# Decode attention in one inference step: block selection ahead of the window branch, bias by one-hot products, lists loaded from two queues

## The chip, the core and the metric

One core of a Trainium2 chip runs the whole program in one launch. The metric is device time in microseconds (us) of one execution; the time of a kernel is the median of its runs. A core has TensorE (PE in the profile), VectorE (DVE), ScalarE (ACT), GpSimd (POOL) and SyncE (SP). Each has its own instruction queue, and they meet only at semaphores. Sixteen DMA engines are shared by all; a load is issued by the queue of SP, ACT or POOL.

## What is computed

The kernel is one layer of a hybrid decoder, run for a prompt of 1024 tokens and for eight sequences (`B = 8`) that each add one token to a cache of 8192. Only the attention of those eight new tokens is touched by the change. It has three branches, each with a bias that depends on distance; `BG = 16` pairs of sequence and key/value group, four query heads each:

```python
s_c = einsum(q, kc) + bias_c;  p_c = softmax(s_c);  o_c = p_c @ vc          # 511 compressed blocks
imp = sum(p_c, heads) @ block_cover                                          # importance of 129 blocks of 64 tokens
score = where(valid, where(forced, BIG, imp), NEG)                           # first, last and current block forced
_, idx = top_k(score, 16)                                                    # a list of 16 blocks per pair
k_sel, v_sel = ks_blk[b, g, idx], vs_blk[b, g, idx]                          # gathered from the paged cache
s_s = einsum(q, k_sel) + table[rel_bucket(qpos - kpos)];  o_s = softmax(s_s) @ v_sel
s_w = einsum(q, kw) + bias_w;  o_w = softmax(s_w) @ vw                       # window of 512
o = gate_c * o_c + gate_s * o_s + gate_w * o_w
```

The bias depends on the distance in buckets; beyond 790 tokens it is one value, the last bucket.

## The kernel before

The program is a row of stages with a barrier of all engines between two; `decode_attention` (L1878) is one of them, after the attention of the prompt and before `merge`. Nothing of the next stage runs in it. Rows of the score matrix `S` (64 partitions) are sequence and head; its columns are 512 compressed, 512 window and 1024 selected keys.

**SP** (L1930) issues all plain loads: compressed keys `kcT` (2 MB in one), window rows `win` (8 of 512 KB), the page table `pti`, gates `gt`, compressed values `vc`, and later, per list, the one row of the new token into the gathered block (L1945), after the list's gathers have landed.

**POOL** (L1949) makes constants, then issues 16 indirect gathers of bias rows into `bsel` (L1969), then 8 indirect gathers per list into `kvs` (L1977): 128 rows of 1 KB each, keys and values of both groups. `kvs` has two slots; a slot is free when PE has turned it (`s_sT`) and ACT has copied its values (`s_vs`).

**PE** (L2094): scores of the compressed keys (L2099); then per sequence the window's keys are turned (`win_turn`, L2107) and multiplied (L2115); importance (L2118); two small products that spread indices (L2120, L2121); per list 8 turns (`sel_turn`, L2131) and two score products (`sel_scores`, L2141), each two rows of the trace; then 16 turns of `S` (L2154) and 256 value products (L2167), all 128 of one group (partitions 0 to 63 of the bank), then all of the other (64 to 127). A product is two instructions in the trace.

**DVE** (L1980), in this order: window copies (L1993), compressed softmax (L1995 to L2000), selection (L2003 to L2012), block numbers to row numbers by 16 pairs of one-hot and sum (L2022, L2025), row numbers `gidx` (L2040), window maximum, per list two copies of turned keys (L2052), then maximum, factors and scaling of all three branches (L2055 to L2072), and the last copy into `oaT` (L2077). ACT does the exponentials (L2084, L2086, L2092) and the copies of values (L2090).

## Time and profile before

| | us |
|---|---|
| median of 3 runs | 3674.04 (3670.31 to 3681.82) |
| the profiled execution, device time | 3669.99 |
| its span in the trace | 3668.4 |
| the stage `decode_attention`, 2023.41 to 2332.70 of the span | 309.3 |

Over the whole span TensorE is busy 83%, and the granted clock is 0.873 of full speed. In this stage it is another picture, so the shares of the page say little here: the stage has to be read in stretches, with the timeline for the starts and the stretches' table for busy time, granted clock and DMA. "Granted clock" is the share of 2.4 GHz that TensorE got: 0.50 is its lower level of 1.2 GHz, 1.00 the upper.

### The profile page before, as it was taken

The numbers are of one execution on the slowest core, as the hardware profiler recorded it, in microseconds if no ns is written. First come the engines' busy times: TensorE is split into PE (matmuls) and PEld (weight loads), VectorE is DVE, ScalarE is ACT, GpSimd is POOL, SyncE is SP. The second block draws the span as 40 slices with busy tenths as digits, with TensorE's granted clock in tenths as the row PEclk, the third lists the DMA queues.
The fourth block names the chain that finished last, engine by engine and source line by source line (L and its number), as shares of the span: only waits on it lengthen the run. The fifth ranks groups of instructions, "written<-read, shape, count | busy, mean of one in ns | idle before, by whom it ended". The sixth has DMA issues, their size and how long they took to land. (4 is left out here: it accounts for less than half of the span.)

```text
span 3668.4 us, 48382 instructions
## 1 busy us (share of the span) xinstructions
PE 3050.1 (83%) x17167; PEld 2645.7 (72%) x17167; DVE 1508.2 (41%) x3336; ACT 1134.4 (31%) x2011; POOL 620.3 (17%) x983
## 2 busy tenths in 40 slices
PE   4799979998497649599999356899986799999996
PEld 3677758786395449577777123888875799999995
DVE  3456546564414640144555311111133444444446
ACT  3577757774421211143344000111112211111112
POOL 6556546650001000000000374000000000000000
PEclk9899989998798859777788655699998899999998
DMA  9778768871413233300000332411122211111111
GB/s 120 103 114 117 113 100 122 119 109 59 161 42 116 95 103 127 100 18 12 6 12 0 111 105 63 139 46 40 29 87 99 69 46 57 34 51 51 34 34 46
DMA packets 268889, 276.13 MB, mean 75 GB/s; under 512 B 51738, under 2 KB 224270, under 8 KB 268088
## 3 DMA queue, kind: packets, MB, share of 16 engines
q1 hardware_dynamic: 209470, 180.94, 18.2%
q0 software_dynamic: 43520, 67.82, 11.5%
q10 hardware_dynamic: 15738, 25.40, 3.9%
q8 instruction: 79, 1.29, 0.2%
q14 instruction: 82, 0.67, 0.1%
HBM read 241.17 MB, written 36.71 MB: 76 GB/s over the span
## 5 line engine op out<-in xcount | busy, mean ns | idle before, releaser
L232 POOL DMA_DIRECT2D raw<-in_cache_nsa_kv x768 | 457.0, 595 | 348.1 <-issue 307.1
L2193 PE MATMUL bank<-u2H,fwiH 128*128 128x344 f32 x1056 | 338.3, 320 | 39.2 <-DVE fwiL L2560 39.2
L405 ACT ACTIVATE cy<-bank 64x512 f32<-64x512 f32 x512 | 303.0, 592 | 116.9 <-PE bank L286 109.9
L2193 PE MATMUL bank<-u2H,fwiL 128*128 128x344 f32 x1056 | 337.9, 320 | 0.0
L2193 PE MATMUL bank<-u2L,fwiH 128*128 128x344 f32 x1056 | 337.7, 320 | 0.0
L2193 PE MATMUL bank<-cxH,cwH 128*128 128x512 f32 x768 | 324.5, 423 | 3.3 <-DVE cxL L517 3.3
L2193 PE MATMUL bank<-cxH,cwL 128*128 128x512 f32 x768 | 307.0, 400 | 0.0
L2193 PE MATMUL bank<-cxL,cwH 128*128 128x512 f32 x768 | 306.8, 399 | 0.0
L2193 PEld LDWEIGHTS bank<-u2H,fwiH 128*128 128x128 f32 x1056 | 199.5, 189 | 39.7 <-issue 39.7
L2193 PEld LDWEIGHTS bank<-u2H,fwiL 128*128 128x128 f32 x1056 | 199.2, 189 | 0.0
L2193 PEld LDWEIGHTS bank<-u2L,fwiH 128*128 128x128 f32 x1056 | 198.7, 188 | 0.0
L2193 PEld LDWEIGHTS bank<-cxH,cwH 128*128 128x128 f32 x768 | 147.5, 192 | 51.6 <-issue 15.0
L2568 DVE TENSOR_TENSOR fhm<-bank,fsl 128x344 f32<-128x344 f32 x66 | 34.1, 517 | 344.0 <-ACT fsl L2543 344.0
L286 PE MATMUL bank<-ident,raw 128*128 128x128 f32 x1024 | 140.4, 282 | 42.2 <-DMA raw<-in_cache_nsa_kv 39.9
L2193 PE MATMUL bank<-guH,gwgH 128*128 128x344 f32 x480 | 160.9, 335 | 14.7 <-DMA guL<-uL_d 14.7
L2193 PEld LDWEIGHTS bank<-cxH,cwL 128*128 128x128 f32 x768 | 146.5, 191 | 35.2
L2184 DVE SCALAR_TENSOR_TENSOR xT<-bank,modT,xT 128x344 f32<-128x344 f32 (+1 forms) x264 | 148.6, 570 | 53.2 <-PE bank L2193 53.2
L286 PEld LDWEIGHTS bank<-ident,raw 128*128 128x128 f32 x1024 | 124.6, 146 | 63.5 <-issue 42.8
L2193 PE MATMUL bank<-fhH,fwoL 128*128 128x344 f32 x528 | 169.7, 321 | 0.0
L2193 PE MATMUL bank<-fhH,fwoH 128*128 128x344 f32 x528 | 168.9, 320 | 0.0
L2193 PE MATMUL bank<-fhL,fwoH 128*128 128x344 f32 x528 | 168.9, 320 | 0.0
L2193 PEld LDWEIGHTS bank<-cxL,cwH 128*128 128x128 f32 x768 | 147.5, 192 | 25.9
(479 smaller groups left out, 6411.3 us busy)
## 6 DMA issues: line engine op xcount, KB each, us to landing
raw<-in_cache_nsa_kv POOLq DMA_DIRECT2D x768, 64.0 KB, 8.2
fwi<-in_w_ffn_in SPq DMA_DIRECT2D x44, 512.0 KB
raw<-in_cache_nsa_kv SPq DMA_DIRECT2D x256, 64.0 KB
wada<-in_w_ada ACTq DMA_DIRECT2D x8, 2048.0 KB
fwo<-in_w_ffn_out SPq DMA_DIRECT2D x22, 512.0 KB
gwg<-in_w_in SPq DMA_DIRECT2D x20, 512.0 KB
mwada<-in_w_ada SPq DMA_DIRECT2D x4, 2048.0 KB, 9.0
mwada<-in_w_ada_final SPq DMA_DIRECT2D x4, 2048.0 KB, 8.0
```

The source lines that it names most:

```text
L232: eng.dma_start(raw[8 * q:8 * q + 8, t % 2, nt], pages[bass.ds(at[n], 1), :, :, P * kv:P * kv + P] .rearrange("o n s c -> (o n) s c")).the ...
L286: mm = pe.transpose(k.bank[6 + odd][:, P * nt:P * nt + P], raw[:, t % 2, nt, 2 * j + odd, :], k.ident[:, :])
L405: ins = act.activation(y[HD * odd:HD * odd + HD, kk % 3, 0:2, g, 0:HP], k.bank[6 + odd][HD * g:HD * g + HD, :].rearrange("p (i r) -> p r i ...
L2184: dve.scalar_tensor_tensor(out=x, in0=bank[:, 0:w], scalar=k.modT[:, bass.ds(gate + c, 1), 0:1].rearrange("p o b -> p (o b)"), in1=x, op0= ...
L2193: mm = pe.matmul(out, a[x], b[y], start=start and n == 0, stop=stop and n == 2)
L2568: dve.tensor_tensor(hm[:, u % 2, :], k.bank[2 * (u % 2) + 1][:, 0:GT], sl[:, u % 2, :], ALU.mult).then_inc(s_hm, 1)
```

## The change

Only `decode_attention` is changed.

- **Order.** The compressed softmax, the selection and the row numbers now come ahead of the window branch on PE and DVE. Small conversions that don't depend on the selection are done before it. The 16 pairs of one-hot and sum are staggered by one. The window's turned keys are copied by ACT instead of DVE. `kcT` comes in four loads; `win` and `vc` are issued by ACT.
- **Bias.** The 16 gathers of `bsel` are gone. 28 small loads bring the bias of the 14 nearest blocks (`near`) less the far value, a one-hot matrix `oh` says which block stands where, and 16 products (L2210) add the bias into the score banks after the first list. The far value is the same for all keys of a head and drops out of the softmax.
- **Lists.** Blocks 0 to 7 of a list are loaded by SP, with a page address read from `tix` into registers (8 plain loads of 64 rows per list, L1966); blocks 8 to 15 by 4 indirect gathers of POOL (L1999), the last of 64 rows. The new token's row is loaded by SP beside them. `kvs` has three slots instead of two.
- **Other branches during the loads.** Window maximum, exponential and factors, the first 8 turns of `S` and the value products of the compressed and window branches (128 products over lists 6 to 13) stand between the lists. The selected branch's own value products (128) stay behind the last list. In both, the two groups now alternate product by product.

On SP, the queue of a list. Before, this was one row of 1 KB per list; the whole queue of the stage was:

```order
L1932 DMA kcT<-kcT_d 128x4096
L1934 DMA dwin<-out_win_sample 128x4x256 x8
L1937 DMA dpti<-in_page_table 1x64 x16
L1939 DMA dgt<-smalltok_d 8x3 x8
L1940 DMA vc<-vc_d 128x4096
L1945 DMA dkvs<-out_kv_sample 1x256 x16
```

Now, from the last pair of bias loads to the first of list 0's blocks (ISA is the address arithmetic):

```order
L1948 DMA dnear<-biasrev_d 8x64
L1949 DMA dfar<-biasrev_d 8x2
L1958 DMA dkvs<-out_kv_sample 1x256
L1962 TENSOR_LOAD dtix
L1966 ISA
L1966 DMA dkvs<-in_cache_nsa_kv 64x256
```

The last two rows come eight times per list, and the four rows from L1958 on begin each of the 16 lists.

On DVE, the front of the stage, before:

```order
L1986 COPY qpad<-qTs 64x8x4 x2
L1993 COPY dwT<-bank 128x512 x8
L1995 ISA dS,dmx<-bank,bias_cmp 64x512
L1995 ISA dmx 64x1
L1996 TENSOR_SCALAR dnm<-dmx 64x1
```

and now:

```order
L2009 COPY qpad<-qTs 64x8x4 x2
L2012 CAST diota<-diti 16x128
L2013 CAST dcolf<-dcoli 128x1
L2014 CAST dwho<-dwi 128x64
L2015 TENSOR_SCALAR dprow<-dcolf 128x1
L2016 TENSOR_SCALAR dprow<-dprow 64x1
L2019 TENSOR_SCALAR dtokb<-dpti 16x64 x2
L2022 ISA dS,dmx<-bank,bias_cmp 64x512
```

The maximum over the compressed scores (L1995, now L2022) no longer stands behind eight copies of the window branch.

On PE, the end of the stage, before (the last three rows come 16 times):

```order
L2131 MATMUL bank<-ident,dkvs 128x128 x8
L2141 MATMUL bank<-dsT,qpad 64x512 x4
L2154 MATMUL bank<-ident,dS 128x64 x16
L2167 MATMUL bank<-dpT,vc 64x4 x4
L2167 MATMUL bank<-dpT,dwin 64x4 x4
L2167 MATMUL bank<-dpT,dvsel 64x4 x8
```

and now, from the last value products that stand between lists:

```order
L2233 MATMUL bank<-dpT,vc 64x4 x8
L2233 MATMUL bank<-dpT,dwin 64x4 x8
L2194 MATMUL bank<-ident,dkvs 128x128 x8
L2204 MATMUL bank<-dsT,qpad 64x512 x2
L2194 MATMUL bank<-ident,dkvs 128x128 x8
L2204 MATMUL bank<-dsT,qpad 64x512 x4
L2221 MATMUL bank<-ident,dS 128x64 x8
L2233 MATMUL bank<-dpT,dvsel 64x4 x128
```

Half of the turns and half of the value products have left the end.

The core of the diff:

```diff
+    RING = 3
+    NEAR = PAST // SEL - 13
...
         def _(sp):
-            sp.dma_start(kcT[:, :, :], k.kcT_d).then_inc(s_kc, 16)
-            for b in range(B):
-                sp.dma_start(win[:, b], k.o["win_sample"]...).then_inc(s_win, 16)
+            for j in range(4):
+                sp.dma_start(kcT[:, 2 * j:2 * j + 2, :], k.kcT_d[:, 2 * j:2 * j + 2, :]).then_inc(s_kc[j], 16)
...
-            sp.dma_start(vc[:, :, :, :], k.vc_d).then_inc(s_vc, 16)
+            for n in range(14):
+                sp.dma_start(near[H * n:H * n + H, :], k.biasrev_d[0:H, SEL * (NEAR + n):SEL * (NEAR + n + 1)]).then_inc(s_bias, 16)
+                sp.dma_start(far[H * n:H * n + H, :], k.biasrev_d[0:H, 0:2]).then_inc(s_bias, 16)
...
             for bg in range(BG):
-                sp.wait_ge(s_ga[bg % 2], 128 * (bg // 2 + 1))
-                sp.dma_start(kvs[64:65, bg % 2, 7, :], new[bg // 2:bg // 2 + 1, 256:512]).then_inc(s_new[bg % 2], 16)
+                r = bg % RING
+                if bg >= RING:
+                    sp.wait_ge(s_sT, 2 * (bg - RING + 1))
+                    sp.wait_ge(s_vs, bg - RING + 1)
+                sp.dma_start(kvs[64:65, r, 7, :], new[bg // 2:bg // 2 + 1, 256:512]).then_inc(s_blk[r], 16)
+                if bg == 0:
+                    sp.wait_ge(s_idx, 3)
+                at = nc.values_load_multi_w_load_instructions(tix[0:1, TOPN * bg:TOPN * bg + 8], ...)[1]
+                for n in range(8):
+                    sp.dma_start(kvs[64 * (n % 2):64 * (n % 2) + 64, r, n // 2, :], tokens[bass.ds(at[n], SEL), 256:512]).then_inc(s_blk[r], 16)
...
         def _(pool):
-            pool.wait_ge(s_bidx, 1)
-            for n in range(TOPN):
-                pool.indirect_dma_start(out=bsel[:, SEL * n:SEL * n + SEL], ...).then_inc(s_bg, 16)
             pool.wait_ge(s_idx, 2)
             for bg in range(BG):
-                if bg >= 2:
-                    pool.wait_ge(s_sT, 2 * (bg - 1))
-                    pool.wait_ge(s_vs, bg - 1)
-                for m in range(8):
-                    pool.indirect_dma_start(out=kvs[:, bg % 2, m, :], ...).then_inc(s_ga[bg % 2], 16)
+                if bg >= RING:
+                    pool.wait_ge(s_sT, 2 * (bg - RING + 1))
+                    pool.wait_ge(s_vs, bg - RING + 1)
+                for m in range(4, 8):
+                    n = P if m < 7 else 64
+                    pool.indirect_dma_start(out=kvs[0:n, r, m, :], ...).then_inc(s_ga[r], 16)
...
         def _(dve):
+            dve.memset(kvs[64:P, :, 7, :], 0.0).then_inc(s_z, 1)
...
-            dve.tensor_scalar(bidx[:, :], k.bank[5][0:64, 0:TOPN], hrow[:, :], None, ALU.add).then_inc(s_bidx, 1)
+            dve.tensor_scalar(tix[:, :], k.bank[6][0:1, 0:BG * TOPN], 0.5, None, ALU.mult).then_inc(s_idx, 1)
+            dve.tensor_tensor(yr[:, :, :], ..., ALU.mult).then_inc(s_ix, 1)
+            for a in range(2):
+                dve.tensor_tensor(oh[:, 8 * a:8 * a + 8, :], k.bank[4 * a][0:112, :]..., ALU.is_equal).then_inc(s_oh, 1)
...
+                if bg == 2:
+                    window()
+                if bg == 3:
+                    window_factors()
+                if bg == 4:
+                    turned(0)
...
         def _(act):
+            for b in range(B):
+                act.dma_start(win[:, b], k.o["win_sample"]...).then_inc(s_win, 16)
+            act.dma_start(vc[:, :, :, :], k.vc_d).then_inc(s_vc, 16)
             act.wait_ge(s_gt, 16 * B)
             act.activation(gt[:, :], gt[:, :], ACT.Sigmoid).then_inc(s_sig, 1)
...
         def _(pe):
+            def values(b, sel):
+                for n in range(8):
+                    for g in range(G):
+                        ...
+                        mm = pe.matmul(k.bank[1 if sel else 4][HD * g:HD * g + HD, 4 * b:4 * b + 4], v,
+                                       pT[:, 8 * sel + n, 8 * b + 4 * g:8 * b + 4 * g + 4], start=(n == 0), stop=(n == 7))
...
             for bg in range(BG):
                 sel_turn(bg)
                 if bg:
                     sel_scores(bg - 1)
+                if bg == 4:
+                    rows_turn(0)
+                if bg >= 6 and bg < 6 + B:
+                    mm = values(bg - 6, 0)
             sel_scores(BG - 1)
+            rows_turn(1)
+            for b in range(B):
+                mm = values(b, 1)
```

## Rows read from the trace of the kernel before

**Rows 1.** Stretches of the stage: busy time, instructions, granted clock, DMA.

```profile
core 0: us, PE busy (x) PEld busy (x) DVE busy (x) ACT busy (x) POOL busy (x), PEclk, DMA share, GB/s
2023.00:2041.00 18.00, 9.56 (x16) 2.66 (x16) 0.37 (x2) 1.28 (x1) 1.77 (x9) 0.72 0.96 331
2041.00:2056.00 15.00, 13.22 (x47) 5.72 (x48) 5.77 (x9) 1.49 (x2) 0.00 (x0) 0.89 0.45 165
2056.00:2107.00 51.00, 3.42 (x9) 0.90 (x6) 16.23 (x66) 1.63 (x4) 24.47 (x27) 0.54 0.11 28
2107.00:2262.00 155.00, 82.22 (x185) 35.72 (x186) 21.60 (x32) 10.08 (x16) 112.16 (x118) 0.50 0.34 101
2262.00:2278.00 16.00, 8.90 (x24) 2.96 (x22) 5.97 (x18) 1.24 (x2) 0.00 (x0) 0.50 0.01 2
2278.00:2333.00 55.00, 54.37 (x512) 54.28 (x512) 0.24 (x2) 0.00 (x0) 0.00 (x0) 0.50 0.00 1
```

**Rows 2.** Timeline of POOL; start, us, line, [idle before <-releaser].

```profile
2074.61 1.00 POOL L1969 DMA_INDIRECT dbsel<-biasrev_d,dbidx  x1 [49.25 <-DVE dbidx L2036]
...
2253.28 0.95 POOL L1977 DMA_INDIRECT dkvs<-in_cache_nsa_kv,dgidx  x1 [0.30 <-issue]
```

**Rows 3.** Line L1977: duration ns min/median/max, first and last start; time to landing.

```profile
L1977 POOL DMA_INDIRECT dkvs<-in_cache_nsa_kv,dgidx x128: 947/953/972, 2094.2 to 2255.8; - x128
...
DMA to landing us min/median/max: 2.6/2.8/3.7
```

**Rows 4.** Timeline, the front of the stage.

```profile
2023.41 0.33 SPq L1932 DMA_DIRECT2D kcT<-kcT_d  x1
...
2030.86 9.56 PE L2099 MATMUL bank<-kcT,qpad 128*64 128x512 f32 x16 [9.74 <-DMA kcT<-kcT_d]
...
2055.77 0.68 DVE L1995 CUSTOM_DVE_ANT_0 dS<-bank,bias_cmp 64x512 f32<-64x512 f32 x1
...
2074.95 0.73 DVE L2040 TENSOR_SCALAR dgidx<-bank,dprow 64x128 uint32<-64x128 f32 x2 [0.63 <-PE bank L2121]
```

**Rows 5.** SP's issues by line: duration ns min/median/max, first and last start.

```profile
L225 SPq TENSOR_LOAD <-pt x32: 692/1069/1367, 2.4 to 777.0; - x32
L232 SPq DMA_DIRECT2D raw<-in_cache_nsa_kv x256: 676/692/7371, 3.3 to 805.4; - x128
L232 SPq DMA_DIRECT2D raw<-in_cache_nsa_kv x2: 676/676/676, 7.1 to 8.0; - x2
L1652 SPq DMA_DIRECT2D strip<-biasfwd_d x8: 333/338/538, 1559.7 to 1890.5; - x8
L1934 SPq DMA_DIRECT2D dwin<-out_win_sample x8: 427/1389/3372, 2023.8 to 2033.9; - x8
L1945 SPq DMA_DIRECT2D dkvs<-out_kv_sample x16: 222/223/237, 2105.7 to 2258.5; - x16
```

**Rows 6.** Timeline of PE: a list's turns and scores; window scores at the upper clock.

```profile
2259.72 1.97 PE L2131 MATMUL bank<-ident,dkvs 128*128 128x128 f32 x8 [4.16 <-DMA dkvs<-out_kv_sample]
...
2265.44 3.64 PE L2141 MATMUL bank<-dsT,qpad 64*64 64x512 f32 x4
...
2050.17 1.07 PE L2115 MATMUL bank<-dwT,qpad 128*64 128x512 f32 x2
```

**Rows 7.** A stretch of the prompt's attention, columns as in rows 1.

```profile
1570.00:1610.00 40.00, 40.00 (x122) 28.57 (x120) 15.02 (x66) 11.75 (x38) 0.00 (x0) 0.50 0.00 1
```

**Rows 8.** Timeline of PE where value products pass from one group to the other.

```profile
2305.10 0.25 PE L2167 MATMUL bank<-dpT,dvsel 128*64 128x4 f32 x1
2305.13 0.25 PE L2167 MATMUL bank<-dpT,vc 128*64 128x4 f32 x1
...
2305.21 0.25 PE L2167 MATMUL bank<-dpT,dvsel 128*64 128x4 f32 x1
```

**Rows 9.** Timeline, the end of the stage.

```profile
2278.10 1.01 PE L2167 MATMUL bank<-dpT,vc 128*64 128x4 f32 x8 [0.78 <-DVE dpT L2075]
...
2332.51 0.19 DVE L2077 COPY oaT<-bank 128x32 f32<-128x32 f32 x1 [54.47 <-PE bank L2167]
```

More of the change, by code:

```diff
@@ L1921, in decode_attention @@
         gidx = k.sb("dgidx", [P, BG, 8], U32, ctx=ctx)
-        bidx = k.sb("dbidx", [64, TOPN], U32, ctx=ctx)
-        bsel = k.sb("dbsel", [64, NSELK], ctx=ctx)
-        kvs = k.sb("dkvs", [P, 2, 8, 256], ctx=ctx)
+        tix = k.sb("dtix", [1, BG * TOPN], I32, ctx=ctx)
+        yr = k.sb("dyr", [BG, TOPN, 64], ctx=ctx)
+        near = k.sb("dnear", [112, SEL], ctx=ctx)
+        far = k.sb("dfar", [112, 2], ctx=ctx)
+        oh = k.sb("doh", [112, TOPN, 64], ctx=ctx)
+        kvs = k.sb("dkvs", [P, RING, 8, 256], ctx=ctx)
         sT = k.sb("dsT", [P, 2, NSELK], ctx=ctx)
@@ L1939, in _ @@
                 sp.dma_start(gt[8 * b:8 * b + 8, :], k.smalltok_d[b, 0:24].rearrange("(h r) -> h r", r=3)).then_inc(s_gt, 16)
-            sp.dma_start(vc[:, :, :, :], k.vc_d).then_inc(s_vc, 16)
+            for n in range(14):
+                sp.dma_start(near[H * n:H * n + H, :], k.biasrev_d[0:H, SEL * (NEAR + n):SEL * (NEAR + n + 1)]).then_inc(s_bias, 16)
+                sp.dma_start(far[H * n:H * n + H, :], k.biasrev_d[0:H, 0:2]).then_inc(s_bias, 16)
             new = k.o["kv_sample"][0].rearrange("b o v g d -> b (o v g d)")
+            sp.wait_ge(s_z, 1)
             for bg in range(BG):
-                sp.wait_ge(s_ga[bg % 2], 128 * (bg // 2 + 1))
-                sp.dma_start(kvs[64:65, bg % 2, 7, :], new[bg // 2:bg // 2 + 1, 256:512]).then_inc(s_new[bg % 2], 16)
-            for j in range(2):
-                sp.wait_ge(s_new[j], 8 * BG)
+                r = bg % RING
[4 more added lines that the diff above has]
+                if bg == 0:
+                    nc.disable_value_cache = True
+                    sp.wait_ge(s_idx, 3)
+                at = nc.values_load_multi_w_load_instructions(
+                    tix[0:1, TOPN * bg:TOPN * bg + 8], engines=(mybir.EngineType.SP,), min_val=0, max_val=POOL * PAGE - SEL,
+                    skip_runtime_bounds_check_because="a page number of the table, by its meaning, and a half of the page")[1]
+                for n in range(8):
+                    sp.dma_start(kvs[64 * (n % 2):64 * (n % 2) + 64, r, n // 2, :], tokens[bass.ds(at[n], SEL), 256:512]).then_inc(s_blk[r], 16)
+            nc.disable_value_cache = False
+            for j in range(RING):
+                sp.wait_ge(s_blk[j], 144 * len(range(j, BG, RING)))
         @block.gpsimd
@@ new lines, in _ @@
+            for bg in range(BG):
+                g, r = bg % 2, bg % RING
+                act.wait_ge(s_ga[r], 64 * (bg // RING + 1))
+                act.wait_ge(s_blk[r], 144 * (bg // RING + 1))
+                act.activation(vsel[:, bg], kvs[:, r, :, P + HD * g:P + HD * g + HD], ACT.Copy).then_inc(s_vs, 1)
+                if bg == 2:
+                    act.wait_ge(s_nm, 2)
+                    act.activation(S[:, 512:1024], S[:, 512:1024], ACT.Exp, bias=nm[:, 1:2], accum_out=ls[:, 1:2]).then_inc(s_exp, 1)
@@ L2094, in _ @@
+            act.wait_ge(s_nm, 3)
+            for a in range(2):
+                ins = act.activation(S[:, 1024 + 512 * a:1536 + 512 * a], k.bank[5 + a][0:64, :], ACT.Exp, bias=nm[:, 2:3], accum_out=ls[:, 2 + a:3 + a])
+            ins.then_inc(s_exp, 1)
         @block.tensor
@@ L2096, in _ @@
             pe.wait_ge(s_qp, 2)
-            pe.wait_ge(s_kc, 16)
             for b in range(B):
+                if b % 2 == 0:
+                    pe.wait_ge(s_kc[b // 2], 16)
                 mm = pe.matmul(k.bank[0][0:64, :], qp[:, 64 * b:64 * b + 64], kcT[:, b, :], start=(b == 0), stop=(b == B - 1))
             mm.then_inc(s_sc, 1)
-            pe.wait_ge(s_win, 16 * B)
+            pe.wait_ge(s_const, 8)
+            pe.wait_ge(s_p, 1)
+            pe.matmul(k.bank[4][0:BG, :], gsel[:, :], S[:, 0:512], start=True, stop=True).then_inc(s_imp, 1)
+            pe.wait_ge(s_ix, 1)
+            pe.matmul(k.bank[6][:, 0:BG * TOPN], k.ones[0:BG, :], tbd[:, :, :].rearrange("p n m -> p (n m)"), start=True, stop=True).then_inc(s_imp, 1)
+            pe.wait_ge(s_ix, 2)
+            for a in range(2):
+                pe.matmul(k.bank[4 * a][0:112, :], k.ones[0:BG, 0:112], yr[:, 8 * a:8 * a + 8, :].rearrange("p n r -> p (n r)"),
+                          start=True, stop=True).then_inc(s_y, 1)
             def win_turn(b):
```

202 lines of the change are left out of this document (111 added, 91 removed).

## The prediction

> **What bounds the kernel now.** I read the stage in stretches first, then the starts of the work that ends each stretch. It runs from 2023.41 to 2332.70 [rows 4, 9], 309.3 us of the span, and four limits follow one another in it.
>
> The front, to 2094.2, moves no cache rows. The compressed scores end on PE at 2030.86 + 9.56 = 2040.42, but DVE starts on their maximum only at 2055.77, because the window's eight copies stand ahead of it in its queue; selection to row numbers then takes until 2074.95 + 0.73 = 2075.68 [rows 4]. POOL's first gather is at 2074.61, and 16 gathers of bias keep it from the lists until 2094.2 [rows 2, 3].
>
> The loop of 16 lists is POOL's: 128 gathers start between 2094.2 and 2255.8 [rows 3], each 0.95 us with 0.30 of idle time between two [rows 2], so 10.06 us a list. DMA engines are busy 0.34 there, PE 82 of 155 us, at granted clock 0.50 [rows 1].
>
> Then the softmax over the selected keys, from 2265.44 + 3.64 = 2269.08 [rows 6] to the first value product at 2278.10 [rows 9]: 9.0 us. Last 512 value instructions in 54.4 us [rows 1], 0.1066 us each, with PE alone.
>
> **The change part by part.** *Front.* DVE no longer waits behind the window: the maximum starts when the compressed scores end. Their keys now share the DMA engines with the window's rows, which ACT issues at the same time. Shared evenly, 2.1 MB of keys arrive with 2.1 MB of others at 331 GB/s [rows 1]: 12.7 us instead of 6.3, so the last quarter lands near 2037 instead of 2030.86, and its four score rows follow, 3.6 us at the lower clock by the four of a list [rows 6], less at the upper: 2040.4, the old end. Without contention it would be 2037; with the loads crowding out the keys, 2044. ACT issues nine loads, at a median 1.39 us [rows 5] some 12.5 us, before the gates' sigmoid and the exponential: done at about 2036, ahead of 2041. Gain 15.3 us. The chain from the maximum to the row numbers, 19.9 us [rows 4], I keep whole: what leaves it and what its staggered pairs hide, 1 to 3 us, stays as margin. First gather 2040.4 + 19.9 + 0.3 = 2060.6; SP, after `tix` and a register load, 2061.7. The bias gathers, 2094.2 - 2074.6 = 19.5 us [rows 2, 3], are gone from POOL. Their replacement: 28 small loads on SP, 0.22 to 0.36 us each [rows 5], 6 to 10 us, behind which only SP's own lists stand, and these wait for `tix` until 2061: nothing. The one-hot matrix on DVE (three operations of about 0.7 to 1.3 us) lies beside PE's window branch: nothing, and if it were late, list 0's scores would be by as much. On PE 16 bias products, 32 instructions of 64 columns at about 0.12 us, an estimate from the 0.107 of rows 1: 3.9 us after list 0.
>
> *Window branch.* It moves behind the selection on PE: 3 us for the one-hot's products, then the 15 us of before (2041 to 2056) [rows 1]; PE reaches list 0 at 2061 + 18 - 1 = 2078. Queued behind it: turns and, on ACT, copies of values of lists 0 to 2, so slots come free late and lists 3 on start some 2 us later than they could.
>
> *Loading a list.* POOL: 4 x 1.25 = 5.0 us. SP: eight loads, a register load, one row. The trace has no load of 64 rows of 1 KB from a register's address. Nearest below: 128 rows of 4 KB with such an address, 0.34 us (L1652); above: 128 pieces of 512 bytes, 0.68 (L232), and these follow one another at 0.9, so 0.2 lies between [rows 5]. I take 0.34 + 0.2, since the pieces are few and long: 8 x 0.54 + 0.22 + 0.1 + 0.69 to 1.07 = 5.5 us. By the upper row: 8 x 0.9 + 1.07 + 0.3 = 8.6. Both ends are under 10.06. Lists by SP alone would end at 2061.7 + 16 x 5.5 + 2 = 2152.
>
> The DMA engines were the lesser concern: at 101 GB/s they are busy 0.34 [rows 1]; a list of 1 MB in 5.5 us is 191 GB/s, below the 331 of the front. The Trainium skill (DMA: Bandwidth & Descriptors, Rules for kernel authors) says that spreading loads over SP, ACT and GpSimd gains no bandwidth, and that two transfers to disjoint halves of the partitions serialize; by that rule a list could not be faster than its bytes allow. At the front's 331 GB/s that is 3.2 us, which would end nothing here.
>
> *PE in the loop.* A list is 1.97 us of turns and 3.64 of scores [rows 6], 5.6 us; that was half hidden under 10.06 and now is as long as the load. Into it come 8 turns (1.0 us) and eight times 32 value instructions. If the two groups run side by side these cost 0.053 each, 1.7 us a list. The trace shows that once, where one group ends: products of the two, 0.03 us apart, each at 0.11 [rows 8]. At the lower clock the loop is 16 x 5.6 + 3.9 + 1.0 + 8 x 1.7 = 108 us. It enters from the window branch at the upper clock, where score rows take half (1.07 for two [rows 6]); I take off 4 us for that. 2078 + 104 = 2182, later than the loads' 2152: PE ends the loop.
>
> *Which clock.* Here the two readings part. In the prompt's attention, with 64-row score products and turns as here, PE was busy 40 of 40 us and the clock stayed at 0.50 [rows 7]; the old loop had 0.50, too, and the value products ran 54 us at 0.50 [rows 1]. I take 0.50.
>
> *End.* Of the 9.0 us, two scalings of `S`, eight turns and one copy of turned rows go, and the exponential is in two parts: 6.6, an estimate. Value products: 256 x 0.053 = 13.7 us instead of 54.4. Last addition 0.4. End of the stage 2182 + 6.6 + 13.7 + 0.4 = 2202.7, before 2332.7: 130 us less. The barrier behind the stage hands all of it on. From the profiled execution, 3669.99 - 130 = 3540; that execution lies 4 us under the median of the runs shown, which gives 3544 against it, and I put the forecast at **3541**.
>
> **Rivals.** *The clock rises.* The loop's work now has hardly a gap. Then a list costs PE about 3 us and the loads end the loop: 2061.7 + 88 + 2 + 2.8 to land, one turn and two lists of scores 4.6, end 20: 2179, 154 us less, **3518**; with SP at POOL's 5.0 us, 3510. For it: the window branch, as dense, came to 0.89 [rows 1]. Against: rows 7. The Trainium skill (TensorE: Matmul & The Clock Gate, Why this matters for your kernels) advises keeping TensorE busy without a break so that it gets the upper clock; by that rule this would be the forecast, and rows 7 speak against it for this mix of shapes.
>
> *Value products don't pair.* Then 0.107 each: 8 x 1.7 more in the loop and 13.7 more at the end, 27 us: **3568**. For it: rows 8 are a few instructions, and here both groups follow in one stream for hundreds. The Trainium skill (the same page, The mechanism) says that a weight load overlaps running products only when the row group differs, and here both groups use all rows; by that rule this is the result. Rows 8 are against it.
>
> *SP's loads are slow.* At 8.6 us a list the loads end the loop: 2061.7 + 138 + 2.8 + 2.0 + two lists of scores 7.3, end 20.7: 2232, 100 us less, **3570**. For it: row L232, the only one that loads the same cache by the same means.
>
> *Slower than before.* SP's issue is held by its queue: the same line L232 took up to 7.37 us [rows 5]. Every list waits for SP, so this decides from 14.9 us a list (2061.7 + 16 x 14.9 + 12.1 + 20.7 = 2332.7), which is 1.5 us an issue besides the 0.2 between. At 2.0 us, 19 us a list, the stage ends at 2399: **3740**. Against: that row stands in a stretch where several queues fill the DMA engines; here they have half their time left.
>
> *Nothing gained.* The stage would have to keep 10 us a list; no row gives a price for that but the last rival at one point.
>
> **How the numbers follow.** Forecast 0.47; clock rises 0.23; no pairing 0.13; SP slow 0.12; slower 0.04; no effect 0.01. The first four are all faster by over 0.3% (11 us, about what a measurement of this kernel can tell from no change): faster 0.95, same 0.01, slower 0.04. The forecast's own spread is the front's +4 and -3, 1 to 3 us of the chain, and the part of the loop at the upper clock, 3525 to 3552. The range takes in the three faster rivals with the bounds of SP's pace, 3508 to 3574; outside lie SP slower still, and two of the late cases together.
>
> **What would show it.** Right: the compressed maximum by 2044, first gather by 2063, no `bsel`; starts of lists 5 to 6 us apart in lists 1 to 5 and near 7.3 in 6 to 13, with PE the one waited for and clock 0.50; SP's loads 0.3 to 0.4 us; last value products 14 us. Clock at 1.00 in the loop shows the first rival, 27 us of last products the second, ACT and PE waiting for SP's loads with gaps of 3 us the third. The forecast is wrong if keys land after 2045, if DVE or ACT hold the slots (a third party I cost at nothing: per list DVE has 21.6 / 16 = 1.4 us, ACT 10.1 / 16 = 0.6 [rows 1], and the window's maximum and factors come to DVE once), or if POOL's gathers slow beside SP's.

## The result

The changed kernel takes 3549.93 us (median of 4 runs, 3538.05 to 3555.70) beside 3672.18 us for the one before on the same chip: a ratio of 0.9658, 95% interval 0.9626 to 0.9691. The forecast was 3541, its range 3508 to 3574. The profiled execution has a span of 3544.3 us. Its decode stage begins at 2028.66 and ends at 2208.76, 180.1 us long; it was 309.3 [rows 4, 9]. The forecast had 179.3.

One thing has to be known for everything below. The code ahead of the stage is the same in all kernels here, yet the stage began anywhere between 2002.85 and 2048.12 us in the profiled executions. A few us in the stage therefore can't be read from the time of a single run; I compare the length of the stage within each profile, from POOL's first memset (`qpad<-`) to the end of DVE's last addition or copy (`oaT<-bank`), and use whole times where there are several runs. The changed kernel's own stage is 180.1 us in one profile and 180.7 in another (changed_again below), so differences of that size are not read.

The stage after, in stretches, with the columns of [rows 1]:

```profile
core 0: us, PE busy (x) PEld busy (x) DVE busy (x) ACT busy (x) POOL busy (x), PEclk, DMA share, GB/s
2028.00:2043.00 15.00, 8.94 (x16) 2.38 (x16) 2.46 (x11) 0.00 (x0) 1.92 (x10) 0.77 0.91 300
2043.00:2066.00 23.00, 3.08 (x4) 0.63 (x4) 14.78 (x58) 3.58 (x5) 0.67 (x1) 0.58 0.49 172
...
2084.00:2094.00 10.00, 8.97 (x65) 5.42 (x64) 4.17 (x7) 1.24 (x3) 6.08 (x7) 1.00 0.45 132
2094.00:2104.00 10.00, 5.77 (x23) 3.16 (x22) 4.01 (x12) 1.97 (x4) 7.56 (x9) 0.87 0.57 166
2104.00:2187.00 83.00, 82.10 (x404) 41.81 (x402) 16.52 (x25) 6.92 (x11) 35.45 (x38) 0.50 0.41 122
...
2194.00:2209.00 15.00, 13.82 (x256) 13.73 (x256) 0.84 (x2) 0.00 (x0) 0.00 (x0) 0.50 0.01 3
```

Against [rows 1], the 51 us in which PE was idle and POOL gathered bias rows have become 23; the 155 us of lists, with PE half idle, are 103, the last 83 of them with PE busy for 82.1 us but at clock 0.50; and the 55 us of value products are 14.

The front after, from the timeline (start, us, engine, line; idle time before it and what ended that in brackets), to be read beside [rows 4]:

```profile
2028.66 0.58 POOL L1973 MEMSET qpad<- 128x576 f32 x1 [130.07 <-POOLq L135]
2028.67 13.45 ACTq L2128 DMA_DIRECT2D dwin<-out_win_sample  x8
...
2033.05 8.94 PE L2158 MATMUL bank<-kcT,qpad 128*64 128x512 f32 x16 [6.08 <-DMA kcT<-kcT_d]
...
2040.06 0.19 PEld L2158 LDWEIGHTS bank<-kcT,qpad 128*64 128x64 f32 x2 [0.80 <-DMA kcT<-kcT_d]
...
2042.14 1.54 ACTq L2129 DMA_DIRECT2D vc<-vc_d  x1
...
2042.41 0.40 DVE L2019 TENSOR_SCALAR dtokb<-dpti 16x64 f32<-16x64 int32 x2 [10.61 <-DMA dpti<-in_page_table]
...
2042.85 0.68 DVE L2022 CUSTOM_DVE_ANT_0 dS<-bank,bias_cmp 64x512 f32<-64x512 f32 x1
...
2043.72 1.28 ACT L2131 ACT_TABLE_LOAD   x1 [34.54 <-issue]
...
2045.24 1.28 ACT L2133 ACT_TABLE_LOAD   x1
...
2047.38 0.15 DVE L2025 TENSOR_SCALAR dmx<-dls 64x1 f32<-64x1 f32 x1 [3.66 <-ACT dS L2133]
...
2065.33 1.07 POOL L1999 DMA_INDIRECT dkvs<-in_cache_nsa_kv,dgidx  x1 [34.57 <-DVE dgidx L2058]
```

The maximum of the compressed scores starts 14.2 us into the stage (32.4 before), the first gather of a list at 36.7 (70.8 before [rows 3, 4]). The scores themselves end at 13.3; the 0.9 us between are the conversion of the page table (L2019), which now stands ahead of the maximum on DVE and waited 10.61 us for its loads. A new wait shows, of 3.66 us: DVE stands until ACT's exponential is through, and ACT comes to it late, behind nine DMA issues, a sigmoid and two table loads.

Issues of a list by line, as in [rows 5] (duration in ns min/median/max, first and last start): the register load, the eight blocks, the new row on SP, and POOL's gathers.

```profile
L1962 SPq TENSOR_LOAD <-dtix x16: 732/751/803, 2065.5 to 2167.8; - x16
...
L1966 SPq DMA_DIRECT2D dkvs<-in_cache_nsa_kv x128: 468/469/1219, 2066.4 to 2174.1; - x128
...
L1958 SPq DMA_DIRECT2D dkvs<-out_kv_sample x16: 249/402/460, 2048.9 to 2167.3; - x16
...
L1999 POOL DMA_INDIRECT dkvs<-in_cache_nsa_kv,dgidx x64: 905/953/1097, 2065.3 to 2164.5; - x64
```

SP's sixteen register loads lie between 2065.5 and 2167.8, so a list costs it 102.3 / 15 = 6.8 us; in the undisturbed lists 6.6 (two loads at 2073.12 and 2079.69). The waits of the stage say who stood for whom (us in total, times, longest):

```profile
POOL dkvs L1999 <- PE bank L2194: 22.6, 8, 5.8
...
SPq L1958 <- PE bank L2194: 1.1, 2, 1.0
```

POOL stood 22.6 us for free slots, SP 1.1: SP ran at its own speed to the end.

PE in the loop and behind it, from the timeline: turns are L2194, scores L2204, bias products L2210, value products L2233.

```profile
2084.73 1.09 PE L2194 MATMUL bank<-ident,dkvs 128*128 128x128 f32 x8
...
2089.70 2.08 PE L2210 MATMUL bank<-dnear,doh 112*64 112x64 f32 x32
...
2095.71 1.93 PE L2204 MATMUL bank<-dsT,qpad 64*64 64x512 f32 x4
2101.82 1.94 PE L2194 MATMUL bank<-ident,dkvs 128*128 128x128 f32 x8 [4.18 <-issue]
2103.68 3.67 PE L2204 MATMUL bank<-dsT,qpad 64*64 64x512 f32 x4
...
2114.65 1.94 PE L2194 MATMUL bank<-ident,dkvs 128*128 128x128 f32 x8 [0.75 <-issue]
...
2120.12 1.02 PE L2233 MATMUL bank<-dpT,vc 128*64 128x4 f32 x16
...
2121.93 1.97 PE L2194 MATMUL bank<-ident,dkvs 128*128 128x128 f32 x8
...
2184.30 3.64 PE L2204 MATMUL bank<-dsT,qpad 64*64 64x512 f32 x4
...
2194.69 13.82 PE L2233 MATMUL bank<-dpT,dvsel 128*64 128x4 f32 x256 [0.78 <-DVE dpT L2090]
```

Lists 0 to 2 have scores of 1.93 us, the upper clock. Then PE catches up with the loads and stands 4.18 us for list 4. The turns and scores behind that wait (2101.82, 2103.68) are at the lower clock, and to the end of the stage each list's scores take 3.64 to 3.67. Lists with value products are 7.3 us apart (2114.65 to 2121.93).

### The profile page after: what moved, and what is told of

It reads as the page before. It is cut to its first block and busy times, and to the rows that moved or that the text cites. A ratio compares the mean times of both kernels' runs of the same rounds, so it can differ in the third digit from the quotient of the medians.

```text
span 3544.3 us, 48834 instructions
## 1 busy us (share of the span) xinstructions
PE 3023.0 (85%) x17201; PEld 2620.6 (74%) x17201; DVE 1505.1 (42%) x3334; ACT 1138.9 (32%) x2021; POOL 544.5 (15%) x904
```

## The experiments

Length of the stage in each profile, by the rule above; whole times where there are several runs.

| run | stage, us | against | difference | whole kernel, us |
|---|---|---|---|---|
| before | 309.3 | | | 3672.18 |
| changed | 180.1 | before | -129.2 | 3549.93 |
| values_apart | 200.0 | changed | +19.9 | 3569.17 |
| before_values_alternate | 283.2 | before | -26.1 | 3645.22 |
| lists_by_pool | 229.1 | changed | +49.0 | 3597.12 |
| sigmoid_late | 177.8 | changed | -2.3 | |
| before_no_bias_gathers | 292.6 | before | -16.7 | |
| window_first | 195.1 | changed | +15.0 | |
| dense_filler | 192.2 | changed | +12.1 | |
| three_fillers | 176.5 | changed | -3.6 | |
| paired_scores | 173.2 | changed | -6.9 | 3541.44 |
| scores_loads_sigmoid | 161.3 | changed | -18.8 | 3530.59 |
| scalar_loads_too | 155.7 | changed | -24.4 | 3528.95 |
| changed_again | 180.7 | changed | +0.6 | 3548.94 |

**Do the value products pair?** The first experiment undoes the alternating order in the changed kernel, the second puts it alone into the kernel before.

```
             def values(b, sel):
-                for n in range(8):
-                    for g in range(G):
+                for g in range(G):
+                    for n in range(8):
```

> The changed kernel with its value products put back in the order of before: all eight of one group, then all eight of the other, so that no two neighbours write different halves of the bank's rows; all else as changed. Theory (the alternating order pairs them): each instruction goes from about 0.054-0.059 us back to the 0.106 us of before; 256 of them stand in the list loop, which PE bounds (+12 us), and 256 behind the softmax (+13.4 us), so the stage is 25 us longer, about 3575 us. Rival (the order brings nothing, the short products of the end come from fewer of them or from another clock): 13.8 us for the 256 at the end as now, the whole within 3 us of the changed kernel.

The last 256 take 21.5 us instead of 13.82 (all of them grouped, then start by start; same columns as above):

```profile
L2233 PE MATMUL bank<-dpT,dvsel 128*64 128x4 f32 x256 | 21.5, 249 | 0.8 <-DVE dpT L2090 0.8
```

```profile
2111.38 0.25 PE L2233 MATMUL bank<-dpT,dwin 128*64 128x4 f32 x1
2111.41 0.25 PE L2233 MATMUL bank<-dpT,vc 128*64 128x4 f32 x1
2111.49 0.25 PE L2233 MATMUL bank<-dpT,dwin 128*64 128x4 f32 x1
```

The ratio to before is 0.97 (0.9668 to 0.9732), the stage 19.9 us longer: the order pays, and the rival falls. The size was 25 and is 20, and the rows show why: where one group's run of 16 instructions meets the next one's, the two run side by side for a few of them (starts 0.03 us apart, then 0.08). In the kernel before such a place came once in 512 instructions [rows 8]; here every 16.

```
-            for g in range(G):
-                for b in range(B):
+            for b in range(B):
+                for n in range(16):
+                    for g in range(G):
...
```

> The kernel before with one part of the change alone: its 512 value products at the end go group by group alternately. Theory: 54.4 us become 512 x 0.054 = 27.6 us, so 3645 us, 27 us less than before. Rival: the pairing needs what else the change made (half of the products early, a sum of two banks); then 54 us stay and the time is that of before.

```profile
2276.85 1.02 PE L2168 MATMUL bank<-dpT,vc 128*64 128x4 f32 x16 [0.78 <-DVE dpT L2075]
...
2302.47 1.85 PE L2168 MATMUL bank<-dpT,dvsel 128*64 128x4 f32 x32
```

It gave 3645.22 us, ratio 0.99 (0.9865 to 0.9934); the 512 products run from 2276.85 to 2304.3, 27.5 us, and their start in the stage moves by 0.8 us only. That is 0.0537 us each; the prediction had 0.053. So 26 us could be had in the kernel before with an exchange of three loops.

**What is SP's half worth?** All gathers by POOL, SP with the new rows only.

```
-                for m in range(4, 8):
+                for m in range(8):
...
-                at = nc.values_load_multi_w_load_instructions(
...
-                for n in range(8):
-                    sp.dma_start(kvs[64 * (n % 2):64 * (n % 2) + 64, r, n // 2, :], tokens[bass.ds(at[n], SEL), 256:512]).then_inc(s_blk[r], 16)
```

> The changed kernel with all 16 lists gathered by POOL (8 gathers of 128 rows each), SyncE loading only the one new row of each list: SyncE's half undone, all else as changed. Theory: POOL needs 8 x (0.953 + 0.30) = 10.0 us a list, more than PE's 7.3, so the loop is bound by loads; the first gather at +36.7 us of the stage, the last issued 160 us later, then landing 2.8, turn 2.0 and scores 1.9 to 3.7, and the 20.9 us of the end as now: stage about 225 to 227 us, 45 us longer than the changed one, about 3595 us. Rival (PE bounds the loop by its clock whatever loads it, and SyncE's half brings little): within 10 us of the changed kernel.

```profile
2157.91 1.97 PE L2185 MATMUL bank<-ident,dkvs 128*128 128x128 f32 x8 [2.68 <-DMA dkvs<-in_cache_nsa_kv,dgidx]
...
2167.89 1.97 PE L2185 MATMUL bank<-ident,dkvs 128*128 128x128 f32 x8 [2.60 <-DMA dkvs<-in_cache_nsa_kv,dgidx]
```

Lists are 10.0 us apart, PE waits for the gathers in each, and the stage is 49 us longer (45 expected; ratio to before 0.9785, 0.9744 to 0.9827). Of the parts that were undone here, SP's half of the lists is the largest.

**What were the bias gathers worth?** The kernel before without them; the bias of the selected blocks is left out, zeros are added.

```
+            pool.memset(bsel[:, :], 0.0).then_inc(s_bg, 16 * TOPN)
             pool.wait_ge(s_bidx, 1)
-            for n in range(TOPN):
-                pool.indirect_dma_start(out=bsel[:, SEL * n:SEL * n + SEL], out_offset=None, in_=brow,
-                                        in_offset=bass.IndirectOffsetOnAxis(ap=bidx[:, n:n + 1], axis=0)).then_inc(s_bg, 16)
```

> The kernel before without its 16 gathers of the bias rows on POOL; the bias of the selected blocks is left out (a buffer of zeros is added instead). Theory: POOL is the bound there, 16 x 1.25 us stood ahead of its first list, so the lists end 20 us earlier and the stage is 289 us instead of 309. Rival (something else of the front end, PE's window products or the index chain, holds the first list): under 10 us gained.

16.7 us, nearer to the theory than to the rival. The first list gather comes at 2087.16 - 2033.82 = 53.3 into the stage instead of 70.8, 17.4 earlier: POOL now waits for the row numbers, which are ready 1.1 us after it began with the bias [rows 2, 4]. The rest is that the 128 gathers are 1.277 us apart there, 1.272 before.

**What is "selection first" worth?** PE's order of before within the changed kernel: the window's turns and products ahead of the importance product.

```
+            pe.wait_ge(s_win, 16 * B)
+            win_turn(0)
...
             pe.wait_ge(s_const, 8)
             pe.wait_ge(s_p, 1)
...
-            pe.wait_ge(s_win, 16 * B)
-            win_turn(0)
```

> The changed kernel with one thing undone, PE's order: the window's turns and products (about 15 us) stand ahead of the importance and index products again, as before the change; loads, lists, values and all other engines' orders as changed. Theory (selection first is worth the window block): the first gather comes at about +50 instead of +36.7 of the stage; PE then has nothing to do while list 0 loads, and the lists, bound by loads up to list 6 and by PE behind it, end 7 to 13 us later: stage 187 to 193 us. Rival (the window block fills time that the first list's landing takes anyway, and PE is the bound of the loop): within 3 us of 180.

```profile
2078.95 1.07 POOL L1999 DMA_INDIRECT dkvs<-in_cache_nsa_kv,dgidx  x1 [50.20 <-DVE dgidx L2058]
```

```profile
2093.82 1.94 PE L2194 MATMUL bank<-ident,dkvs 128*128 128x128 f32 x8 [4.25 <-DMA dkvs<-in_cache_nsa_kv]
2095.69 3.67 PE L2204 MATMUL bank<-dsT,qpad 64*64 64x512 f32 x4
2099.29 3.67 PE L2210 MATMUL bank<-dnear,doh 112*64 112x64 f32 x32
```

First gather at 52.3, near the 50 expected, but the stage is 15.0 us longer where 7 to 13 were expected. The rows show 3.3 us that the expectation didn't have: without the window's block ahead of it, PE enters the lists at the lower clock, and list 0's scores and the bias products take 3.67 us each instead of 1.93 and 2.08. Read with the changed kernel's rows, the block behind the selection does two things: it fills the time of the first loads, and it hands PE on at the upper clock.

**The exponential behind ACT's issues.** The sigmoid and the compressed values' load go behind it.

```
-            act.dma_start(vc[:, :, :, :], k.vc_d).then_inc(s_vc, 16)
-            act.wait_ge(s_gt, 16 * B)
-            act.activation(gt[:, :], gt[:, :], ACT.Sigmoid).then_inc(s_sig, 1)
             act.wait_ge(s_nm, 1)
             act.activation(S[:, 0:512], S[:, 0:512], ACT.Exp, bias=nm[:, 0:1], accum_out=ls[:, 0:1]).then_inc(s_exp, 1)
+            act.dma_start(vc[:, :, :, :], k.vc_d).then_inc(s_vc, 16)
+            act.wait_ge(s_gt, 16 * B)
+            act.activation(gt[:, :], gt[:, :], ACT.Sigmoid).then_inc(s_sig, 1)
```

> The changed kernel with the sigmoid of the gates and the load of the compressed values moved behind the exponential of the compressed scores on ScalarE (the eight window loads stay ahead). Theory: the exponential stood 2.9 us late behind these (load 1.5, table for the sigmoid, sigmoid, table for the exponential 1.3 us); DVE's wait of 3.66 us ahead of the maximum of the sums falls to under 1 us and everything up to the first gather comes about 2.9 us earlier; the stage is 177 us instead of 180. Rival: the exponential then still waits for its table, or the lists' loop takes the gain back: stage 179 to 181 us.

```profile
2028.74 0.72 ACT L2130 ACTIVATE dS<-dS,dnm 64x512 f32<-64x512 f32 x1 [33.94 <-DVE dnm L2023]
...
2029.59 0.15 DVE L2025 TENSOR_SCALAR dmx<-dls 64x1 f32<-64x1 f32 x1 [0.88 <-ACT dS L2130]
```

DVE's wait falls from 3.66 to 0.88 and the stage by 2.3 us. In this profile no table load stands ahead of the exponential any more; the sigmoid's comes later, beside other work.

**What makes the loop's clock?** One dense product that nobody reads behind each list's scores, then three (the diff is of the first; the second has `range(3)`).

```
+                if 1 <= bg < 16:
+                    for _ in range(1):
+                        pe.matmul(k.bank[0][:, :], k.ident[:, :], kcT[:, 0, :], start=True, stop=True)
                 if bg == 4:
                     rows_turn(0)
```

> The changed kernel with one more product of 128 x 128 by 512 columns (the identity by a row of kcT, into a bank that nobody reads) behind the scores of every list from the second on, as work that uses the whole array; nothing else moved. It asks whether the upper clock of lists 0 to 3 can be held. Theory (the low clock of the list loop is lost at the wait of list 4 and isn't won back by what PE does there): the clock is 0.50 from about list 4 to the end as now, a filler costs 1.8 us there (2 x 0.92, the scores' 512 columns) and the loop ends some 20 to 24 us later, stage about 202 us. Rival (it is the sparse work, half of the rows and four-column products, that the low clock follows): with dense work in every list the clock is back at 1.00, a list costs 1.1 + 1.9 + 0.9 + 1.9 = 5.8 us, loads at 6.6 us a list bound the loop, and the stage is 5 us shorter than now, about 175 us.

```profile
2091.84 1.30 PE L2194 MATMUL bank<-ident,dkvs 128*128 128x128 f32 x8 [2.26 <-issue]
2093.07 3.67 PE L2204 MATMUL bank<-dsT,qpad 64*64 64x512 f32 x4
...
2099.91 1.93 PE L2204 MATMUL bank<-dsT,qpad 64*64 64x512 f32 x4
```

```profile
2106.00:2176.00 70.00, 70.00 (x330) 33.47 (x329) 10.80 (x16) 5.04 (x8) 22.64 (x24) 0.50 0.34 100
```

PE was slowed behind a wait again, here of 2.26 us and for list 5, and in the lists with value products one dense product each then didn't bring the upper clock back: 70 of 70 us busy at 0.50. The rival falls as it stood, for the whole loop. But the clock did come back where the dense product, and no value products, stood between two lists: for list 5's scores (2099.91, 1.93 us) and for those of the last two lists, which the changed kernel, without the dense product, runs at 3.64 to 3.67. So the theory's 20 us were too many (12 measured), and what PE computes has a part in it.

> The changed kernel with three products of 128 x 128 by 512 columns that nobody reads behind the scores of every list from the second on (dense_filler had one). At the upper clock a list then costs PE 1.1 + 1.9 + 2.9 + 1.2 = 7.1 us, more than the 6.6 us of a list's loads, so PE has no wait in the loop once it has begun at the upper clock. Theory (the clock falls at PE's wait for loads at list 4 and not for what PE computes): no wait, clock 1.00 through the loop, lists about 7.1 us apart, stage 175 to 190 us. Rival (the lower clock comes in the loop with or without a wait): 1.97 + 3.67 + 6.2 + 1.9 = 13.7 us a list from where it falls, stage 240 to 265 us.

```profile
2066.00:2156.00 90.00, 89.47 (x522) 43.22 (x522) 21.07 (x38) 8.89 (x15) 44.78 (x48) 1.00 0.47 136
```

```profile
2138.76 1.06 PE L2194 MATMUL bank<-ident,dkvs 128*128 128x128 f32 x8 [0.53 <-issue]
```

With 45 useless products the stage is 3.6 us shorter. From list 2 on PE has one wait, of 0.53 us, and the granted clock is 1.00 for 90 us; lists with value products are 6.69 us apart (2098.05 to 2104.74) although each holds 2.8 us of waste. So these lists, with turns, scores and value products, can run at the upper clock, and the rival falls. In the changed kernel it is lost at a wait that PE runs into because at the upper clock it is faster than SP loads. Whether the missing wait or the dense products kept the clock up here, this pair of runs doesn't separate; that one dense product isn't enough in the lists with value products, the first of the two shows. And the run prices the rival "the clock rises" of the prediction: scores end at 2158.5, 155.7 us into the stage, against 159.3. The loads are right behind PE.

**Taking the loop's bounds down.** Scores of two lists in one product; then less for SP and more for POOL; then a third queue.

```
-                    dve.tensor_copy(sT[half, bg % 2, 512 * a:512 * a + 512], k.bank[2 + a][half, :]).then_inc(s_sTs, 1)
+                    dve.tensor_copy(sT[half, bg // 2 % 2, 512 * a:512 * a + 512], k.bank[2 + a][half, :]).then_inc(s_sTs, 1)
...
-                    mm = pe.matmul(k.bank[5 + a][0:64, :], qp[half, 64 * b:64 * b + 64], sT[half, bg % 2, 512 * a:512 * a + 512],
+                    mm = pe.matmul(k.bank[5 + a][0:64, :], qp[:, 64 * b:64 * b + 64], sT[:, b % 2, 512 * a:512 * a + 512],
```

> The changed kernel with the scores of two lists in one product: the keys of group 0 and group 1 of one sample stand in the two halves of the same buffer, and one product with all 128 rows takes the place of two with 64 (q is zero outside its group's columns, so the sum is the same). 32 instructions instead of 64, half of the scores' columns. Theory (PE bounds lists 6 to 13 at 7.31 us with its clock at 0.50): a list costs 1.97 + 1.83 + 1.88 = 5.7 us, SyncE's 6.6 to 6.7 us a list bound the loop now; list 15 is loaded at about +147 of the stage, its turn, copies and the last scores end at about +154 instead of +159.3: stage about 175 us, 5 us less. Rival (fuller products bring the upper clock back): the same bound, but a shorter last list: 8 us less. Rival (PE isn't the bound of the loop, loads are already): stage 179 to 181 us.

```profile
2095.01 1.94 PE L2194 MATMUL bank<-ident,dkvs 128*128 128x128 f32 x8 [5.53 <-DMA dkvs<-in_cache_nsa_kv]
2096.88 3.13 PE L2202 MATMUL bank<-dsT,qpad 128*64 128x512 f32 x4
...
2101.74 1.06 PE L2194 MATMUL bank<-ident,dkvs 128*128 128x128 f32 x8 [1.10 <-issue]
```

Ratio to before 0.9644 (0.9603 to 0.9685), which the whole times alone can't tell from the changed kernel's; the stage is 6.9 us shorter, between the theory's 5 and the first rival's 8. PE now waits for SP's loads: half of its scores' work was worth 7 us and no more. The first rival was right about the clock. It falls at a wait as before (turns of 1.94 us behind 5.53), but it comes back during the next paired scores or right behind them (turns of 1.06 us at 2101.74), and so after each of the six falls between lists 4 and 14. In the changed kernel, with scores over 64 rows, it didn't come back in 83 us.

```
-                    tix[0:1, TOPN * bg:TOPN * bg + 8], engines=(mybir.EngineType.SP,), min_val=0, max_val=POOL * PAGE - SEL,
-                for n in range(8):
+                    tix[0:1, TOPN * bg:TOPN * bg + 6], engines=(mybir.EngineType.SP,), min_val=0, max_val=POOL * PAGE - SEL,
+                for n in range(6):
...
-                for m in range(4, 8):
+                for m in range(3, 8):
```

> Three edits on the changed kernel: the scores of two lists in one product (as in paired_scores), the sigmoid behind the exponential (as in sigmoid_late), and six blocks a list by SyncE and five gathers by POOL instead of eight and four. Theory (SyncE's 6.6 us a list, hidden behind PE in the changed kernel, are eight blocks at 0.64 us and 1.5 us for the row and the register loads): SyncE falls to about 5.4 us a list, POOL rises to 5 x 1.256 = 6.3 us and bounds the loop; 16 x 6.3 + 2.8 + 7.1 us behind the first gather at about +34.4: the loop ends at about +145 instead of +159.3, stage about 166 us, 14 us less than the changed kernel (about 3536 us). Rival (the loop is bound by the traffic of both halves together, not by issue): no less than paired_scores, about 175 us.

Ratio 0.959 (0.9541 to 0.9638), stage 161.3: 18.8 us less, 14 expected. SP's lists are 5.4 us apart (2126.37 to 2131.82), and PE waits for POOL, whose five gathers give 6.3 us a list:

```profile
2141.21 1.97 PE L2194 MATMUL bank<-ident,dkvs 128*128 128x128 f32 x8 [3.84 <-DMA dkvs<-in_cache_nsa_kv,dgidx]
...
2153.74 1.97 PE L2194 MATMUL bank<-ident,dkvs 128*128 128x128 f32 x8 [4.31 <-DMA dkvs<-in_cache_nsa_kv,dgidx]
```

Two lists lie between these turns. Paired scores and the late sigmoid alone gave 6.9 and 2.3 us, so some 9.6 us are the new split of the loads. Issue was the bound, not the traffic of both halves; that rival falls.

```
+            def halves(bg):
+                r = bg % RING
+                if bg >= RING:
+                    act.wait_ge(s_sT, 2 * (bg - RING + 1))
+                at = nc.values_load_multi_w_load_instructions(
+                    tix[0:1, TOPN * bg + 6:TOPN * bg + 8], engines=(mybir.EngineType.Activation,), min_val=0, max_val=POOL * PAGE - SEL,
+                    skip_runtime_bounds_check_because="a page number of the table, by its meaning, and a half of the page")[1]
+                for n in range(6, 8):
+                    act.dma_start(kvs[64 * (n % 2):64 * (n % 2) + 64, r, n // 2, :], tokens[bass.ds(at[n - 6], SEL), 256:512]).then_inc(s_blk[r], 16)
...
+                if bg + RING < BG:
+                    act.wait_ge(s_vs, bg + 1)
+                    halves(bg + RING)
```

> The changed kernel with paired scores and the late sigmoid, and with each list's loads over three queues: six blocks by SyncE, the other two of its eight by ScalarE (with its own register loads, behind its copy of the values of the list three before), four gathers by POOL as now. Theory (with POOL at 6.3 us a list the bound of scores_loads_sigmoid was issue, not traffic): SyncE 5.4 us, POOL 5.0, ScalarE 2.7, PE 5.7 at the lower clock and 3.3 at the upper: the slots of lists 3 on are free from about +54; list 15 is issued at +119 and turned at +128 instead of the +136.5 of scores_loads_sigmoid, the loop ends at about +135, stage about 155 us, 25 us less than the changed kernel's 180.2. Rival (PE at its lower clock, or ScalarE standing at a wait between its copies and its loads, holds the loop at 6 us a list): stage 160 us or more, no less than scores_loads_sigmoid's 161.

> The changed kernel itself, beside scalar_loads_too on one chip: 3550 us by its first runs; stage 180 us, ratio to before 0.966.

```profile
2107.00:2176.00 69.00, 46.96 (x388) 29.21 (x388) 18.24 (x29) 7.57 (x12) 39.60 (x42) 0.75 0.50 153
```

3528.95 us, ratio 0.9597 (0.9573 to 0.9621), beside 3548.94 and 0.966 (0.963 to 0.969) for the changed kernel: about 20 us faster than it, and the intervals don't meet. The stage is 155.7 us, 155 were expected, the shortest here; by whole times this version can't be told from scores_loads_sigmoid. The DMA engines are at 0.50, with 153 GB/s, where the kernel before moved 101 [rows 1]. The Trainium skill (DMA: Bandwidth & Descriptors, Rules for kernel authors) says that spreading DMAs over SP, ACT and GpSimd saves only issue time, not bandwidth; the trace agrees with it here, and issue time was what bound.

## Why the prediction was right, and where it was not

The forecast's mechanism held in its order: first the selection, then loads beside the window's block, then PE as the end of the loop at the lower clock, then a short end. Times from the start of the stage:

| step | forecast, us | measured, us |
|---|---|---|
| compressed scores end | 17.0 | 13.3 |
| their maximum starts | 17.0 | 14.2 |
| from there to the row numbers | 19.9 | 22.2 |
| first gather of a list | 37.2 | 36.7 |
| PE reaches list 0 | 54.6 | 56.1 |
| a list on SP | 5.5 | 6.6 to 6.8 |
| a list on POOL | 5.0 | 5.0 |
| bias products | 3.9 | 2.08 |
| lists with value products, apart | 7.3 | 7.31 |
| last scores end | 158.6 | 159.3 |
| to the first of the last value products | 6.6 | 6.75 |
| last value products | 13.7 | 13.82 |
| the stage | 179.3 | 180.1 |

*Front.* Terms were off and cancelled. The compressed scores ended 3.7 us earlier than forecast: the last quarter of the keys was there 11.4 us into the stage (2040.06) and not 13.6 as by even sharing, and its four rows took 1.9 us at the upper clock instead of 3.4. Of this gain 0.9 us went to the page table's conversion. And ACT's nine issues, which I costed at nothing because they would be done by 2036, took 15.0 us and not 12.5; the step that failed is the cover. I had counted the issues alone and left out two table loads of 1.28 us around the sigmoid, and the work that covered them, the compressed scores, ended earlier than thought. sigmoid_late gives the price: 2.3 us. The 1 to 3 us that I kept as a margin for the staggered pairs and for what leaves the chain didn't come: without that wait the chain is still 19.4 us (sigmoid_late, 2027.84 to 2047.25), against 19.9 before.

*Bias products.* Costed from rows at the lower clock, they ran at the upper one: 2.08 us. Where PE entered the lists at the lower clock, in window_first, they took 3.67, near the 3.9 forecast.

*The loop.* 103.2 us from list 0 to the last scores, 104 forecast, is again two errors that cancel. I took off 4 us for the entry at the upper clock; PE was busy for only 97 us, 7 less than forecast, since four lists' turns, three lists' scores and the bias products ran at it. And I gave PE no waits; it had 6.2 us of them, 4.18 for list 4.

*SP.* This is the term with the real error. I priced a block at 0.34 + 0.2; it took 0.469, and with the register operations and gaps eight take 5.10 us, so 0.64 each, and the register load and the new row bring another 1.5. 6.6 to 6.8 us lie between my two bounds of 5.5 and 8.6, nearer to the lower. I forecast that loads would end at 2152 and PE at 2182, 30 us apart; in truth SP's last blocks were issued at 174.1 - 28.7 = 145.4 us into the stage, and with landing and turns the two ends are about level. That it didn't show in the sum is the luck of PE's 7.3: in paired_scores and three_fillers, where PE is faster, 7 and 4 us are gained and not the 24 that I gave to "the clock rises". Two of my own signs failed with it: SP's loads took 0.469 us and not 0.3 to 0.4, and lists 1 to 5 didn't start 5 to 6 us apart (list 4 came 7.1 us behind list 3, 2094.72 to 2101.82).

*The clock.* The level was right, the reason only half. I took 0.50 from the prompt's attention, as if it were a matter of the shapes alone. The loop began at 1.00 with the same shapes, fell at the wait for list 4 and stayed; with three dense products a list and no such wait it stayed at 1.00. I hadn't seen that the slow loads and the low clock hang together. The shapes have their part all the same: behind the same kind of wait the clock came back with scores over 128 rows (paired_scores), and with scores over 64 rows it didn't.

*Value products.* Right, at 0.054 each at the end and 0.057 in the loop (32 from 2120.12 to 2121.93). My 0.1066 for the kernel before is a slip, 54.4 us by 512 is 0.106; nothing hangs on it. The Trainium skill (TensorE: Matmul & The Clock Gate, The mechanism) would have it that a weight load overlaps only products of another row group; the measured 13.82 us for 256 decides against it for this case. The same page of the Trainium skill (Why this matters for your kernels) says in its row on products of few output rows that outputs on different partitions fall into different column groups and run side by side, and with that the trace agrees: 0.054 us each in the alternating order, 0.106 before.

*What the parts are worth.* Undone one at a time: SP's half 49 us, the order of the value products 20, selection first 15; the bias gathers 17, taken from the kernel before. That makes 101 of 129; the parts share time, so the rest isn't a remainder that belongs to any one of them. The third slot, the value products between the lists, ACT's copies and the four loads of keys were not undone alone and have no price here. Of the 9 us between the forecast and the median, 0.8 are the stage's. In the profiled execution the stage began 5.2 us later than before, with the same code ahead; the rest is scatter of that kind.

*What stays open.* Why some products bring the upper clock back and others don't, and whether the changed kernel's own products would keep it if PE never waited: three_fillers took away the wait and added dense work at once. scalar_loads_too with fillers wasn't tried.

## What to carry to other kernels

Count a queue's whole list, register loads, address arithmetic and gaps included, and compare it with the other engines at their faster clock: an engine that overtakes its loads waits, and here paid for one wait of 4.18 us with half its clock to the end of the stage, because the products behind it didn't bring the clock back. When a bound is moved, price the next one behind it; here three bounds lay within a few us of a list, and taking down one gained 4 to 7 us, taking down all of them 24. Before a large rebuild, try the exchange of loops that costs nothing: products that write different halves of the partitions, one after the other, gave 26 us by themselves.

## What the runs showed that I had not expected

- PE can be busy for 82.1 of 83 us at granted clock 0.50 (the lower of its two levels, 1.2 GHz), and 45 added products that nobody reads made the stage 3.6 us shorter, because the clock stayed at 1.00 (2.4 GHz).
- Value products needn't alternate strictly to gain: in runs of 16 instructions a group they took 0.084 us each, alternately 0.054, in one run of 256 a group 0.106 [rows 1].
- An upper clock lost at a wait came back with the next scores over 128 rows, six times of six in paired_scores; with scores over 64 rows in the changed kernel it stayed at 0.50 to the end.
- A load of 64 rows of 1 KB with an address from a register holds SP 0.469 us, 0.64 with what stands around it; the load of eight such numbers into registers 0.75 us. The new row's issue rose from 0.22 us [rows 5] to 0.40.
- The start of the stage moved by 45 us between executions with the same code ahead of it.
